# Six groups of the feed-forward down map by Strassen's scheme, on one Trainium2 core

## What is computed

```python
f = jnp.square(jax.nn.relu(x @ w1 + b1)) @ w2 + b2
x = layer_norm(DN_ALPHA * x + f, ln3_g, ln3_b)
```

## Time and profile before

| what | us |
|---|---|
| median of three runs (1410.17 to 1412.05) | 1411.23 |
| the profiled execution's own time | 1413.16 |
| its span, first to last instruction | 1411.4 |
| TensorE busy | 1362.4 |
| VectorE busy | 717.0 |
| GpSimd busy | 662.9 |
| ScalarE busy | 362.1 |

### The profile page before, as it was taken

How to read it: one execution, slowest core, us unless ns; L and a number is a source line. 1 busy time by engine, 2 the same in 40 slices (tenths; PEclk the granted TensorE clock), 3 DMA queues, 4 the chain that set the end, 5 groups by cost and what they waited for, 6 DMA issues and landing times.

```text
span 1411.4 us, 20758 instructions
## 1 busy us (share of the span) xinstructions
PE 1362.4 (97%) x8456; PEld 1316.5 (93%) x8456; DVE 717.0 (51%) x856; ACT 362.1 (26%) x696; POOL 662.9 (47%) x435
## 2 busy tenths in 40 slices
PE   6999989998899999989999999999999999999996
PEld 6999978798899978989999999999999999999995
DVE  5899994357413743496662125521155311454466
ACT  4222432334512531154320002200022100222233
POOL 3476987345832724549233333333333333334522
PEclk9999999999999999999999999999999999999998
DMA  8223432110110375101111111111111111111112
GB/s 251 68 49 82 117 126 76 30 45 16 30 45 30 118 256 194 60 0 49 42 45 46 45 45 45 45 46 45 45 47 47 50 50 46 46 45 50 56 45 79
DMA packets 44417, 93.55 MB, mean 66 GB/s; under 512 B 20288, under 2 KB 26688, under 8 KB 41920
## 3 DMA queue, kind: packets, MB, share of 16 engines
q1 hardware_dynamic: 34592, 89.73, 20.1%
q10 hardware_dynamic: 9760, 2.93, 0.8%
HBM read 85.39 MB, written 7.25 MB: 66 GB/s over the span
## 4 chain that ended last, share of the span: by engine, by line
PE 76%; DVE 16%; POOL 3%; issue 2%; ACT 1%; DMA 1%; DVEq 0%; SPq 0%; ACTq 0%; POOLq 0%
PE bank L670 23%; PE bank L671 23%; PE bank L672 23%; DVE conv_sum L1694 11%; POOL x_low L570 1%; DVE x_low L1681 1%; POOL w_low L370 1%; PE conv_sum L992 1%; PE bank L967 1%; ACT x_full L1444 1%; PE conv_sum L821 1%; DVE bank L1821 0%; PE conv_sum L672 0%; PE conv_sum L670 0%; PE conv_sum L671 0%
## 5 line engine op out<-in xcount | busy, mean ns | idle before, releaser
L670 PE MATMUL bank<-x_high,w_high 128*128 128x384 f32 (+1 forms) x1200 | 391.8, 327 | 12.7 <-POOL w_low L370 11.5
L671 PE MATMUL bank<-x_low,w_high 128*128 128x384 f32 (+1 forms) x1200 | 389.0, 324 | 0.0
L672 PE MATMUL bank<-x_high,w_low 128*128 128x384 f32 (+1 forms) x1200 | 388.5, 324 | 0.0
L368 POOL TENSOR_TENSOR w_high<-w_raw,ones 128x1024 fp32r<-128x1024 f32 x75 | 142.8, 1904 | 442.5 <-issue 220.9
L670 PE MATMUL bank<-mix,w_high 128*128 128x384 f32 (+1 forms) x832 | 272.7, 328 | 3.4 <-issue 1.9
L671 PE MATMUL bank<-mix,w_high 128*128 128x384 f32 (+1 forms) x832 | 272.8, 328 | 0.0
L672 PE MATMUL bank<-mix,w_low 128*128 128x384 f32 (+1 forms) x832 | 270.6, 325 | 0.0
L670 PEld LDWEIGHTS bank<-x_high,w_high 128*128 128x128 f32 x1200 | 226.7, 189 | 13.7 <-POOL w_low L370 10.3
L671 PEld LDWEIGHTS bank<-x_low,w_high 128*128 128x128 f32 x1200 | 226.8, 189 | 0.1
L672 PEld LDWEIGHTS bank<-x_high,w_low 128*128 128x128 f32 x1200 | 226.6, 189 | 0.0
L370 POOL TENSOR_TENSOR w_low<-w_raw,w_high 128x1024 fp32r<-128x1024 f32 x75 | 183.6, 2448 | 5.9
(11 more groups left out here) (287 smaller groups left out, 1973.9 us busy)
## 6 DMA issues: line engine op xcount, KB each, us to landing
w_raw<-slabs_in SPq DMA_DIRECT2D x110, 512.0 KB, 3.6
dec_kv<-dec_kv_in SPq DMA_DIRECT2D x16, 1024.0 KB, 5.3
scratch<-slabs_in SPq DMA_DIRECT2D x8, 512.0 KB, 3.7
yT_res<-ffn_sum SPq DMA_DIRECT2D x4, 768.0 KB, 3.5
x_full<-xT_in SPq DMA_DIRECT2D x4, 384.0 KB, 5.4
x_full<-xT_in SPq DMA_DIRECT2D x2, 768.0 KB, 9.3
x_full<-xT_in SPq DMA_DIRECT2D x2, 576.0 KB, 11.3
yT_res<-ffn_sum SPq DMA_DIRECT2D x4, 288.0 KB, 2.5
```

What stands on the lines that cost most here:

```text
L368: pool.tensor_tensor(high[:, slot, :], raw[:, p, :], one, ALU.mult).then_inc(high_done, 1)
L670: pe.matmul(out, w_high, x_high, start=first, stop=False)
L671: pe.matmul(out, w_high, x_low, start=False, stop=False)
L672: return pe.matmul(out, w_low, x_high, start=False, stop=last)
```

## The change

The four alternating groups become three stages: all 32 slabs of the up map, then a stage `ST` for hidden rows 0 to 3071 of the down map, then the last eight hidden blocks as before.

In `ST` there are six groups (512 hidden rows each, `GROUPS`) with four units each (`UNITS`; a unit makes two output blocks). A unit is a 2 x 2 product in blocks: the weight quarters b11, b12, b21, b22 (256 hidden rows by 128 outputs each) and the hidden quarters (256 rows by 528 tokens, `HT`). Strassen's scheme makes it with seven products in place of eight, on sums of quarters. A product i takes weight form i and hidden form i; each is a quarter or a sum of quarters, and each is split in high and low parts. One product is 2 halves of 264 tokens x 2 row blocks x 3 matmuls = 12 matmuls, in one pair of PSUM banks; four pairs are used in turn, and eight slots of weight forms.

- VectorE: `unit_weight_sums` makes a unit's four weight sums (256 columns each) two units ahead, from `w_raw`, into two buffers; `form_sums` makes the four sums of hidden forms (1056 elements) for the next group, in units 1 and 2 of a group; `add_product` adds each product onto its target (528 elements); in the last group `join` combines the partial sums, and `join_first` and `join_last` finish them in the last stage.
- ScalarE: `w_form_high` casts each weight form, `form_high` each hidden form of the next group (units 2 and 3).
- GpSimd: `w_form_low` makes the low part of each weight form, `form_low` those of all seven hidden forms: three in unit 3, four in unit 0 of the next group. The low part is written over the full form, so it waits for all four form sums.
- SyncE: `hidden_out` writes each hidden block to a DRAM tensor `hidden` (the last eight as high and low parts), `forms_in` reads a group's four quarters back, `last_hidden_in` the last eight blocks; the load of the unit after the next waits for the current unit's sixth low part.

relu has two buffers, now squared in place and freed by the write to DRAM. ScalarE's copy and VectorE's subtraction per hidden chunk go away; for the last eight blocks they are made per block. Some semaphores are renamed and shared with higher counts. The diff, cut to its core:

```diff
+UP = FF // P
+S_ST = S_FF + UP
+GROUPS, UNITS = 6, 4
+NU = GROUPS * UNITS
 LAST = NSLAB - NB
+LATE = LAST - NU
+HT = T // 2
+FORMS = ("11", "s2", "s1", "s3", "s4", "12", "22")
+FORM_HIGHS = (0, 2, 5, 6, 3, 1, 4)
+KEPT = UP - NB
...
+    forms_high = [at(f"form_high{i}", [P, 7, 2, HT], f32r, o) for i, o in enumerate((O_Q, O_XH))]
+    forms_low = [at(f"form_low{i}", [P, 7, 2, HT], f32r, o + 14 * HT * 4) for i, o in enumerate((O_Q, O_XH))]
+    forms_full = [at(f"form_full{i}", [P, 7, 2, HT], f32, o + 14 * HT * 4) for i, o in enumerate((O_Q, O_XH))]
...
+    weight_sums = at("weight_sums", [P, 2, 3, 256], f32, O_KV + NB * T * 4 + 2 * T * 4)
+    relu_low = at("relu_low", [P, 2, T], f32r, O_KV + NB * T * 4)
+    unit_high = at("unit_high", [P, 2, T], f32r, O_Q + 28 * HT * 4)
...
+    def weight_source(U, i):
+        quarter = {0: 0, 3: 1, 4: 3, 5: 2}
+        if i in quarter:
+            return raw[:, U % 2, quarter[i] * 256:(quarter[i] + 1) * 256]
+        return weight_sums[:, U % 2, {2: 0, 1: 1, 6: 2}[i], :]
+    def unit_raw(U):
+        n = S_ST + U
+        return sem(f"raw_in{U % 2}"), 16 * (n // 2 + 1 - MEM_SLABS // 4)
...
+    def pair(f):
+        k = 2 * (f % 4)
+        return banks[:, k:k + 2, 0:HT // 2]
...
-        loads(S_XO + 8, NSLAB)
+        def hidden_out(j):
+            p = j % 2
+            sp.wait_ge(sem("square"), squared(j + 1))
+            block = relu[:, p, :] if j < KEPT else relu_low[:, p, :].bitcast(f32)
+            sp.dma_start(hidden[:, j, :], block).then_inc(sem(f"hidden_out{p}"), 16)
+            if j >= KEPT:
+                sp.dma_start(hidden[:, j + NB, :], unit_high[:, p, :].bitcast(f32)).then_inc(sem(f"hidden_out{p}"), 16)
+        def forms_in(G):
+            b = G % 2
+            if G == 0:
+                for p in range(2):
+                    sp.wait_ge(sem(f"hidden_out{p}"), 32)
+            elif G == 1:
+                sp.wait_ge(used, S_ST)
+                sp.wait_ge(sem("acc_set"), NB)
+                for p in range(2):
+                    sp.wait_ge(sem(f"hidden_out{p}"), 64)
+            else:
+                sp.wait_ge(sem("st_done"), 7 * UNITS * (G - 1))
+            k = 4 * G
+            for i, lo, t in ((6, k + 2, HT), (3, k, HT), (0, k, 0), (5, k + 2, 0)):
+                sp.dma_start(forms_full[b][:, i], hidden[:, lo:lo + 2, t:t + HT]).then_inc(sem("forms_in"), 16)
+        def last_hidden_in(j):
+            for h, n in ((0, UP + j), (1, KEPT + j)):
+                sp.dma_start(q[:, j, h, :].bitcast(f32), hidden[:, n, :]).then_inc(sem("forms_in"), 16)
+        loads(S_XO + 8, S_FF + 4)
+        for j in range(UP):
+            if j < UP - 2:
+                load_next(S_FF + 4 + j)
+            hidden_out(j)
+            if j == 9:
+                forms_in(0)
+        for U in range(NU):
+            sp.wait_ge(sem("w_form_low"), 7 * U + 6)
+            sp.wait_ge(sem("weight_sums"), 4 * (U + 1))
+            load(S_ST + U + 2, U % 2)
+            if U % UNITS == 0 and U // UNITS + 1 < GROUPS:
+                forms_in(U // UNITS + 1)
+            if U == NU - UNITS:
+                sp.wait_ge(sem("st_done"), 7 * (NU - UNITS))
+                for j in range(NB - 1):
+                    last_hidden_in(j)
+        sp.wait_ge(sem("sums_joined"), 4 * UNITS)
+        last_hidden_in(NB - 1)
+        for j in range(2, NB):
+            sp.wait_ge(split_done, LATE + j - 1)
+            load(LAST + j, j % 2)
...
-        splits(S_FF + 4, LAST + 2)
+        def form_low(G, i):
+            f = forms_full[G % 2][:, i]
+            pool.wait_ge(sem("form_sums"), 4 * (G + 1))
+            pool.wait_ge(sem("form_high"), 7 * G + FORM_HIGHS.index(i) + 1)
+            pool.tensor_tensor(forms_low[G % 2][:, i], f, forms_high[G % 2][:, i].bitcast(f32), ALU.subtract)\
+                .then_inc(sem("form_low_pool"), 1)
+        def w_form_low(U, i):
+            f = 7 * U + i
+            pool.wait_ge(sem("w_form_high"), f + 1)
+            pool.tensor_tensor(wl_forms[:, f % 8, :], weight_source(U, i), wh_forms[:, f % 8, :].bitcast(f32), ALU.subtract)\
+                .then_inc(sem("w_form_low"), 1)
+        splits(S_FF + 4, S_FF + 18)
+        form_low(0, 0)
+        form_low(0, 1)
+        splits(S_FF + 18, S_FF + 20)
+        form_low(0, 2)
+        form_low(0, 3)
+        splits(S_FF + 20, S_FF + 22)
+        form_low(0, 4)
+        form_low(0, 5)
+        form_low(0, 6)
+        splits(S_FF + 22, S_ST)
+        for U in range(NU):
+            G = U // UNITS
+            for i in range(7):
+                w_form_low(U, i)
+                if U % UNITS == 3 and G + 1 < GROUPS and i in (2, 4, 6):
+                    form_low(G + 1, i // 2 - 1)
+                if U % UNITS == 0 and G and i in (0, 2, 4, 6):
+                    form_low(G, 3 + i // 2)
+        pool.wait_ge(sem("st_done"), 7 * NU - 4)
+        split(LATE, 0, LAST // 2, MEM_SLABS, freed=S_ST)
+        pool.wait_ge(sem("st_done"), 7 * NU)
+        split(LATE + 1, 1, LAST // 2, MEM_SLABS, freed=S_ST)
...
+        pair_by_chunks("W1", S_FF, x_normed(2), slots=(keep_high[:, 2:4], keep_low[:, 2:4]), after=last_stats(2))
+        pairs("W1", S_FF, 1, UP // 2, x_parts)
+        def unit_product(U, i):
+            G, f, b = U // UNITS, 7 * U + i, U // UNITS % 2
+            if U % UNITS == 0:
+                pe.wait_ge(*form_order(i, G))
+            pe.wait_ge(sem("w_form_low"), f + 1)
+            k = f % 4
+            if f < 4:
+                for n in (2 * k, 2 * k + 1):
+                    take(n, FREED["ST"][n])
             else:
-                first_pair(f"W1{g}", n0, x_parts)
-            pairs(f"W1{g}", n0, 1, 4, x_parts)
-
-            def hidden_ready(c, k, g=g):
-                if k == 0:
-                    pe.wait_ge(sem("hidden_low"), 24 * g + 21)
-                if k == NB - 1:
-                    pe.wait_ge(sem("hidden_low"), 24 * g + 21 + c + 1)
-
-            if g < FFG - 1:
-                first_pair(f"W2{g}", n0 + GB, q_parts, ready=hidden_ready)
-                pairs(f"W2{g}", n0 + GB, 1, 4, q_parts)
+                pe.wait_ge(sem("st_added"), f - 3)
+            for c in range(2):
+                out = ps[2 * k + c][:, 0:HT // 2]
+                t = slice(c * HT // 2, (c + 1) * HT // 2)
+                for kb in range(2):
+                    w = slice(kb * P, (kb + 1) * P)
+                    last = product(out, wh_forms[:, f % 8, w], wl_forms[:, f % 8, w], forms_high[b][:, i, kb, t],
+                                   forms_low[b][:, i, kb, t], kb == 0, kb == 1)
+            last.then_inc(sem("st_done"), 1)
+        for U in range(NU):
+            for i in range(7):
+                unit_product(U, i)
+        def hidden_ready(c, k):
+            if c == 0 and k in (0, NB - 1):
+                pe.wait_ge(sem("forms_in"), 64 * GROUPS + (32 * NB if k else 32 * (NB - 1)))
...
-            take(b, FREED[f"W2{FFG - 1}"][b] + j // 2)
+                pe.wait_ge(split_done, LATE + j + 1)
+            if c == 0 and j < 2:
+                pe.wait_ge(sem("st_added"), 7 * NU - 3 + b // 2)
...
+        def form_high(G, *which):
+            for i in which:
+                if i in (0, 5, 6):
+                    act.wait_ge(sem("forms_in"), 64 * (G + 1))
+                else:
+                    act.wait_ge(sem("form_sums"), 4 * G + {2: 1, 3: 2, 1: 3, 4: 4}[i])
+                act.copy(forms_high[G % 2][:, i], forms_full[G % 2][:, i]).then_inc(sem("form_high"), 1)
+        def w_form_high(U, i):
+            f = 7 * U + i
+            if f < 8:
+                act.wait_ge(used, S_ST - 1 if f < 4 else S_ST)
+            else:
+                act.wait_ge(sem("st_done"), f - 7)
+            if i in (0, 4, 5):
+                act.wait_ge(*unit_raw(U))
+            else:
+                act.wait_ge(sem("weight_sums"), 4 * U + {2: 1, 3: 2, 1: 3, 6: 4}[i])
+            act.copy(wh_forms[:, f % 8, :], weight_source(U, i)).then_inc(sem("w_form_high"), 1)
+        for j in range(UP):
+            p = j % 2
+            for c, (a, z) in enumerate(CHUNKS):
+                b = slab_arrived(act, "W1", S_FF + j, p, c, j // 2)
+                if c == 0 and j >= 2:
+                    act.wait_ge(sem(f"hidden_out{p}"), units_out(j - 2))
+                act.activation(relu[:, p, a:z], ps[b][:, 0:z - a], ACT.Relu, bias=col("b1", j)).then_inc(free[b], 1)
+            if j == 14:
+                form_high(0, *FORM_HIGHS)
+            if j >= KEPT:
+                act.wait_ge(sem("square"), squared(j) + 3)
+                act.copy(unit_high[:, p, :], relu[:, p, :]).then_inc(sem("unit_high"), 1)
+        for U in range(NU):
+            G = U // UNITS
+            for i in range(7):
+                w_form_high(U, i)
+                turn = {(2, 0): 0, (2, 3): 2, (2, 5): 5, (2, 6): 6, (3, 0): 3, (3, 2): 1, (3, 4): 4}.get((U % UNITS, i))
+                if turn is not None and G + 1 < GROUPS:
+                    form_high(G + 1, turn)
...
+        def form_sums(G, *which):
```

(85 more changed lines are left out.)

157 lines of the change are left out of this document (65 added, 92 removed).

## The result

The changed kernel takes **1428.97 us** (1427.11 to 1429.58) against 1411.64 for the kernel before on the same chip: 1.0126 times the time, 95% interval 1.0113 to 1.0139. It is slower by 17.3 us; the forecast was 17.9. Its profiled execution has a span of 1427.8 us, 16.4 longer than before.

What follows compares the result with a forecast made beforehand. TensorE was taken as the bound, busy 97% of the span; TensorE's part -28.1, entry +5, group changes +34, clock +4, joins +2, last stage +1 gave +17.9, so 1429 us; range 1391 to 1449, the forecast's own 1415 to 1443.

Runs made afterwards that it cites:

- the last kernel: VectorE makes a second hidden-form low part per group (the first form's, behind product 15), against the kernel with second-unit weight sums behind products 0 to 2: 1399.17 us, 0.9908.

## What to carry to other kernels

When an engine gets 90% of a period by its own durations, price its losses to shared ports by rows of the engine itself, apart for short and long operations of the other engine: here 0.22 us for a sum of 256 columns and up to 1.09 for one of 1056 made 38 us into 43.5. Follow each queue past every bulk transfer that isn't urgent, and ask at each in-order wait how many results of the engine behind can be buffered: here four products, 6 us. Balance comes after order: the same work gave groups of 48 and of 43 us, depending only on what stood in front of what.

## What was unexpected

- In the last kernel GpSimd and VectorE each work 93% of a group (40.4 and 40.0 of 43 us), and TensorE still loses 2 us of it, waiting for VectorE's adds. Whether some order gets below 42.8 us a group was not tried.
- TensorE kept its full clock through stops of up to 1.7 us in the middle groups and fell behind the idle times of 4.1 and 8.5 us, although shorter pieces made it fall in the earlier trace rows. In the last kernel it also fell behind a single stop of 1.91 us (matmuls 0.22 us apart from 1032.64).
- A weight sum takes up to 2.74 us beside a form part, and 0.42 alone; yet a kernel with most of them shrunk to 16 columns won only 1.7 us a group, for the shrunk ones wait as long.
